# Expert picking of the first token block: one softmax over eight heads, one set of digit instructions, token parts on ScalarE and GpSimd

## The reference

```
q = (xblk @ w_q).reshape(PEER_BLOCK, PEER_HEADS, 2, PEER_DK // 2)   # 8 heads
s1 = einsum('thd,kd->thk', q[:, :, 0], k1); s2 = einsum('thd,kd->thk', q[:, :, 1], k2)   # 128 keys each
t1, i1 = top_k(s1, 16); t2, i2 = top_k(s2, 16)
cand = t1[..., :, None] + t2[..., None, :]            # 256 a head
cidx = i1[..., :, None] * 128 + i2[..., None, :]
top, pos = top_k(cand, 16)
eidx = take_along_axis(cidx, pos)
gate = softmax(top)
act = gelu(einsum('td,thkd->thk', xblk, expert_u[eidx]))
out = einsum('thk,thkd->td', gate * act, expert_v[eidx])
```

## Time and profile before

| | us |
|---|---|
| median of 3 runs | 3845.22 |
| lowest and highest | 3839.84, 3849.98 |
| the profiled execution | 3841.5 |
| its span | 3839.8 |
| PE busy in the span | 3232.0 (84%) |
| DVE busy | 1787.3 (47%) |
| DMA, mean over the span | 284 GB/s |

### The profile page before, as it was taken

One profiled execution on the slowest core, in us unless ns is written; L12 is line 12 of the kernel. 1 busy time (PEld: TensorE's weight loads), 2 busy tenths in 40 slices (PEclk: granted clock), 3 DMA queues, 4 the chain that ended last, 5 costly groups with the idle time before them and its releaser, 6 DMA issues.

```text
span 3839.8 us, 51087 instructions
## 1 busy us (share of the span) xinstructions
PE 3232.0 (84%) x18104; PEld 2209.3 (58%) x18104; DVE 1787.3 (47%) x4186; ACT 622.4 (16%) x1638; POOL 816.7 (21%) x921
## 2 busy tenths in 40 slices
PE   8999999999998899999899999978765666665564
PEld 7767777777776679999788888745410000000000
DVE  2396655555554310003633333358965444444544
ACT  1001222222221100001011110122221111111111
POOL 1000222211211000000122222223233333333332
PEclk9999999999999889999999999979865555555555
DMA  5433323323331358887799999999999999999997
GB/s 188 152 124 126 112 92 108 114 93 107 111 107 68 127 178 294 295 288 259 272 419 419 417 419 417 418 404 417 386 371 418 418 416 418 417 416 414 415 416 305
DMA packets 201143, 1089.73 MB, mean 284 GB/s; under 512 B 27088, under 2 KB 68944, under 8 KB 73616
## 3 DMA queue, kind: packets, MB, share of 16 engines
q0 software_dynamic: 92160, 671.13, 42.6%
q1 hardware_dynamic: 101760, 394.97, 28.9%
q10 hardware_dynamic: 7120, 22.22, 1.5%
HBM read 1056.59 MB, written 31.65 MB: 283 GB/s over the span
## 4 chain that ended last, share of the span: by engine, by line
PE 54%; DMA 29%; DVE 10%; issue 5%; ACT 1%; POOL 1%; DVEq 0%; SPq 0%; ACTq 0%; POOLq 0%
PE psum L497 24%; DMA branches<-in_peer_u,idx 24%; PE psum L561 15%; DMA ring<-in_peer_u,idx 4%; DVE branches L1801 2%; PE psum L921 2%; DVE branches L1355 2%; DVE ring L1801 1%; PE psum L634 1%; PE psum L643 1%; PE psum L640 1%; PE psum L739 1%; PE psum L338 1%; PE psum L620 1%; PE psum L904 1%
## 5 line engine op out<-in xcount | busy, mean ns | idle before, releaser
L1801 DVE CUSTOM_DVE_ANT_0 ring<-ring,psum 128x1024 f32<-128x1024 f32 x480 | 566.8, 1218 | 644.9 <-DMA ring<-in_peer_u,idx 602.8
L497 PE MATMUL psum<-hT,ring 128*128 128x128 f32 (+2 forms) x4800 | 802.5, 328 | 29.1 <-DMA ring<-in_w_glu 10.6
L497 PEld LDWEIGHTS psum<-hT,ring 128*128 128x128 f32 x4800 | 720.0, 196 | 104.0 <-issue 31.5
L904 PE MATMUL psum<-shared,selb 24*128 24x512 bf16 x1280 | 304.0, 524 | 460.8 <-DVE dots L1801 455.9
L904 PEld LDWEIGHTS psum<-shared,selb 24*128 24x128 bf16 x1280 | 56.5, 96 | 1025.9 <-DVE dots L1801 933.0
L561 PE MATMUL psum<-hT,ring 128*128 128x320 f32 x2112 | 626.4, 436 | 9.4 <-DMA ring<-in_w_att 7.8
L561 PEld LDWEIGHTS psum<-hT,ring 128*128 128x128 f32 x2112 | 382.9, 192 | 142.1 <-issue 15.2
L1215 ACT ACTIVATE ge<-dots 128x1 f32<-128x1 f32 x320 | 94.4, 295 | 1493.6 <-DVE dots L1801 1493.6
L497 PE MATMUL psum<-branches,ring 128*128 128x128 f32 (+1 forms) x2048 | 297.1, 304 | 6.4 <-ACT shared L1151 6.4
L1801 DVE CUSTOM_DVE_ANT_0 branches<-branches,psum 128x1024 f32<-128x1024 f32 x160 | 189.0, 1219 | 237.4 <-DMA branches<-in_peer_u,idx 236.0
L497 PEld LDWEIGHTS psum<-branches,ring 128*128 128x128 f32 x2048 | 287.6, 193 | 10.0 <-issue 10.0
(11 more groups left out here) (385 smaller groups left out, 3343.0 us busy)
## 6 DMA issues: line engine op xcount, KB each, us to landing
ring<-in_w_merge SPq DMA_DIRECT2D x160, 1024.0 KB, 5.2
ring<-in_w_head SPq DMA_DIRECT2D x64, 1024.0 KB, 4.9
ring<-in_w_outp SPq DMA_DIRECT2D x32, 1024.0 KB, 7.0
ring<-in_w_pq SPq DMA_DIRECT2D x32, 1024.0 KB, 8.2
ring<-in_w_att SPq DMA_DIRECT2D x24, 1024.0 KB, 5.5
ring<-in_w_mem SPq DMA_DIRECT2D x16, 1024.0 KB, 5.1
ring<-in_w_glu SPq DMA_DIRECT2D x16, 1024.0 KB, 6.5
out_qkv_out<-ring ACTq DMA_DIRECT2D x16, 520.5 KB
```

The lines of the kernel that those rows point to most:

```text
L497: last = mat(out, ring[:, j, (k0 + kt) * P:(k0 + kt + 1) * P], src[:, kt, :], start=kt == 0, stop=kt == kts - 1)
L904: last = mat(ps[q][:, :], selb[32 * q:32 * q + 24, j, :], hb[32 * q:32 * q + 24, g_, :], start=True, stop=True)
L1801: v.tensor_tensor_reduce(out=u, in0=u, in1=x, scale=1.0, scalar=0.0, op0=ALU.mult, op1=ALU.add, accum_out=dots[:, g_, j, half_:half_ + 1]) ...
```

## The change

It has four parts. (1) Both digits are handled by one set of the three instructions, over twice the elements. (2) The exponential, sum, reciprocal and product of the softmax leave the heads: part 2 writes the 16 best sums into `gfull`, and when all eight heads are through, `gates_in` subtracts the maxima, ScalarE makes one exponential over all heads, and `gates_out` writes the gates over them. `picked` now counts a head when its indices are made, and once more for the gates. Both blocks use it. (3) TensorE transposes the index lists after two tiles, multiplies the third, and then transposes the gates; gathers need the index lists alone (`lists_ready` 1 instead of 2). The lists are transposed a second time into a bank nobody reads, to count `summed`. (4) The first block's token parts: ScalarE copies all of the tokens out of PSUM at m = 0 and makes the three parts by one instruction each at m = 0, 4 and 8; GpSimd makes the two subtractions between; the store stands behind m = 8. VectorE's `rest_pair` is used by the second block alone.

```diff
-            for k in range(3):
+            for k in range(2):
                 merge_tile(0, k)
             pe.wait_ge(picked, PH)
-            nc.tensor.transpose(ps[0][:, 0:P], tk0["efull"][:, 0, :], ident[:]).then_inc(summed, SLOTS)
+            nc.tensor.transpose(ps[2][:, 0:P], tk0["efull"][:, 0, :], ident[:]).then_inc(summed, SLOTS - 1)
+            nc.tensor.transpose(ps[0][:, 0:P], tk0["efull"][:, 0, :], ident[:]).then_inc(lists_turned, 1)
+            merge_tile(0, 2)
+            pe.wait_ge(picked, PH + 1)
             nc.tensor.transpose(ps[1][:, 0:P], tk0["gfull"][:, 0, :], ident[:]).then_inc(lists_turned, 1)
+            nc.tensor.transpose(ps[2][:, P:2 * P], tk0["gfull"][:, 0, :], ident[:]).then_inc(summed, 1)
             for k in range(3, 5):
                 merge_tile(0, k)
...
-                pe.wait_ge(picked, 2 * PH)
                 pe.wait_ge(turned_read, 8)
                 for n, name in enumerate(("efull", "gfull")):
+                    pe.wait_ge(picked, 2 * PH + 1 + n)
                     for t in two:
                         w = P if t == 0 else NS
                         last = nc.tensor.transpose(ps[6 + n][:, t * P:t * P + w], tk1[name][0:w, t, :], ident[0:w, 0:w])
-                last.then_inc(lists_turned, 1)
+                    last.then_inc(lists_turned, 1)
...
+            def first_parts(m):
+
+                act.wait_ge(rest_ready, m)
+                if m == 0:
+                    for q in range(4):
+                        act.wait_ge(turned, q + 1)
+                        last = fn(hres0[:, q * 512:(q + 1) * 512], ps[q], ACT.Copy)
+                    last.then_inc(part_taken, 1)
+                    act.wait_ge(part_taken, 1)
+                fn(parts[:, m, :], hres0, ACT.Copy).then_inc(part_taken, 1)
+                if m == 2:
+                    act.wait_ge(part_taken, 4)
+                    act.dma_start(hparts[0:P], parts[:, :, :]).then_inc(parts_out, 16)
...
-                if m == 0:
-                    for n in two:
-                        split_pair(n, 0, 2 * n, N0, (2 * n, 2 * n + 1))
-                    store_parts(1, 0)
-                else:
+                if m:
                     take_scores0(m - 1)
-                if m >= 5 and m % 2:
-                    soften((m - 5) // 2)
+                if m in (0, 4, 8):
+                    first_parts(m // 4)
...
-            soften(6)
-            soften(7)
-            for n in range(3):
-                gate(0, n)
+            gate(0, 0)
+            gate(0, 1)
+            soften(0)
+            gate(0, 2)
...
-                for n in softened(s):
-                    soften(PH + n)
+                if s == LISTS_AT:
+                    soften(1)
...
-                    v.tensor_tensor(gx, top, top[:, :, 0:1].to_broadcast([P, units, TOPK]), ALU.subtract).then_inc(soft_in, 1)
...
-                    for x in two:
-                        st(v.tensor_tensor(eq, fdig[:, x, :].unsqueeze(2).to_broadcast([P, units * TOPK, TOPK]),
-                                           iota16[:].unsqueeze(1).to_broadcast([P, units * TOPK, TOPK]), ALU.is_equal))
-                        st.wait()
-                        e4 = eq.rearrange("p (t k) r -> p t k r", t=units)
-                        st(v.tensor_tensor(e4, e4, tk["i16"][:, x].unsqueeze(2).to_broadcast([P, units, TOPK, TOPK]), ALU.mult))
-                        st.wait()
-                        st(v.tensor_reduce(e12[:, x, :], eq, AX, ALU.add))
-                        st.wait()
-                    st(v.scalar_tensor_tensor(tk["efull"][:, :, at_], e12[:, 0, :].rearrange("p (t k) -> p t k", t=units),
-                                              float(NK), e12[:, 1, :].rearrange("p (t k) -> p t k", t=units), ALU.mult, ALU.add))
-                    dve.wait_ge(soft_out, first + h + 1)
-                    st(v.tensor_reduce(gsum.rearrange("p t n -> p (t n)"), gx, AX, ALU.add))
+                    st(v.tensor_tensor(eq, fdig.rearrange("p x n -> p (x n)").unsqueeze(2).to_broadcast([P, 2 * units * TOPK, TOPK]),
+                                       iota16[:].unsqueeze(1).to_broadcast([P, 2 * units * TOPK, TOPK]), ALU.is_equal))
                     st.wait()
-                    st(v.reciprocal(gsum, gsum))
+                    e4 = eq.rearrange("p (x k) r -> p x k r", x=2 * units)
+                    i4 = tk["i16"].rearrange("p x t k -> p (x t) k")
+                    st(v.tensor_tensor(e4, e4, i4.unsqueeze(2).to_broadcast([P, 2 * units, TOPK, TOPK]), ALU.mult))
                     st.wait()
-                    v.tensor_tensor(tk["gfull"][:, :, at_], gx, gsum.to_broadcast([P, units, TOPK]), ALU.mult).then_inc(picked, 1)
-                    dve.wait_ge(picked, first + h + 1)
+                    st(v.tensor_reduce(e12.rearrange("p x n -> p (x n)"), eq, AX, ALU.add))
+                    st.wait()
+                    v.scalar_tensor_tensor(tk["efull"][:, :, at_], e12[:, 0, :].rearrange("p (t k) -> p t k", t=units),
+                                           float(NK), e12[:, 1, :].rearrange("p (t k) -> p t k", t=units), ALU.mult, ALU.add)\
+                        .then_inc(picked, 1)
+
+            def gates_in(tk, n):
+
+                units = tk["units"]
+                for t in range(units):
+                    top = tk["gfull"][:, t, :].rearrange("p (h k) -> p h k", h=PH)
+                    gx = tk["cand"][:, t, 0:PH * TOPK].rearrange("p (h k) -> p h k", h=PH)
+                    last = v.tensor_tensor(gx, top, top[:, :, 0:1].to_broadcast([P, PH, TOPK]), ALU.subtract)
+                last.then_inc(soft_in, 1)
...
+            def gates_out(tk, n):
+                units = tk["units"]
+                dve.wait_ge(soft_out, n + 1)
+                for t in range(units):
+                    gx = tk["cand"][:, t, 0:PH * TOPK].rearrange("p (h k) -> p h k", h=PH)
+                    st(v.tensor_reduce(tk["gsum"][:, t * PH:(t + 1) * PH, 0], gx, AX, ALU.add))
+                st.wait()
+                st(v.reciprocal(tk["gsum"], tk["gsum"]))
+                st.wait()
+                for t in range(units):
+                    gx = tk["cand"][:, t, 0:PH * TOPK].rearrange("p (h k) -> p h k", h=PH)
+                    last = v.tensor_tensor(tk["gfull"][:, t, :].rearrange("p (h k) -> p h k", h=PH), gx,
+                                           tk["gsum"][:, t * PH:(t + 1) * PH, :].to_broadcast([P, PH, TOPK]), ALU.mult)
+                last.then_inc(picked, 1)
 
             for h in range(PH):
                 for part in range(4):
                     topk_part(tk0, h, part)
+            gates_in(tk0, 0)
+            v.memset(ps[5], 0.0).then_inc(dotted[1], SLOTS)
             dve.wait_ge(lists_turned, 1)
             v.tensor_copy(eT[:, 0:N0], ps[0][:, 0:N0]).then_inc(lists_ready, 1)
+            gates_out(tk0, 0)
+            st(v.memset(ps[4], 0.0))
+            dve.wait_ge(lists_turned, 2)
             v.tensor_copy(gT[:, 0:N0], ps[1][:, 0:N0]).then_inc(lists_ready, 1)
-            st(v.memset(ps[4], 0.0))
-            v.memset(ps[5], 0.0).then_inc(dotted[1], SLOTS)
...
                 elif LAST_TOPK <= s < LISTS_AT:
                     for n in ((0, 1), (2, 3), (4,), (5,), (6,), (7,))[s - LAST_TOPK]:
                         topk_part(tk1, 6 + n // 4, n % 4)
+                    if s == LISTS_AT - 1:
+                        gates_in(tk1, 1)
+                elif s == LISTS_AT:
+                    gates_out(tk1, 1)
                 elif s == LISTS_AT + 1:
-                    dve.wait_ge(lists_turned, 2)
+                    dve.wait_ge(lists_turned, 3)
                     v.tensor_copy(eT[:, N0:], ps[6][:, 0:N1]).then_inc(lists_ready, 1)
+                    dve.wait_ge(lists_turned, 4)
                     v.tensor_copy(gT[:, N0:], ps[7][:, 0:N1]).then_inc(lists_ready, 1)
...
+            for m in two:
+                pool.wait_ge(part_taken, m + 2)
+                if m:
+                    pool.wait_ge(rest_ready, m)
+                g.tensor_tensor(hres0, hres0, parts[:, m, :], ALU.subtract).then_inc(rest_ready, 1)
...
-            pool.wait_ge(lists_ready, 2)
+            pool.wait_ge(lists_ready, 1)
             with pool.Fori(0, 8) as i:
                 gather_pair(i)
-            pool.wait_ge(lists_ready, 4)
+            pool.wait_ge(lists_ready, 3)
```

52 lines of the change are left out of this document (22 added, 30 removed).

## The result

| | before | after |
|---|---|---|
| median of 4 runs each, us | 3847.09 | 3817.76 |
| lowest and highest | 3839.84, 3849.98 | 3815.53, 3822.07 |
| the profiled execution | 3841.5 | 3818.61 |
| its span | 3839.8 | 3816.9 |
| PE, DVE, ACT busy | 3232.0, 1787.3, 622.4 | 3227.9, 1770.1, 605.3 |

The ratio is 0.9928, with a 95% interval of 0.9911 to 0.9945; a later measurement, with 15 runs of the kernel before and 5 of the changed one, gave 0.9944 (0.9931 to 0.9958). The change makes the kernel faster by 0.6 to 0.7%, 21 to 28 us. The forecast was 16 us, and the time lies under its range.

The account below looks back on a forecast made before the run. The DMA flow, hardly resting after the first expert rows and thin from 2720 to 2820, bounds the kernel. 16.2 - 0.5 (contention) - 0.5 (thinner start) + 0.5 (second block) = about 16 us off 3845.2: 3829.2 us, range 3820 to 3839.

Parts of the forecast that it names:

- A head in 8.19 us, no stall in head 0: First block's picking on VectorE: 1.14 us saved a head from 9.33, and head 0's 4.0 us stall gone; 13.1 us.
- The list at 1860.3: End of the first block's picking: head 7's index list ready at about 1860.3 us.
- the contention: GpSimd's second subtraction beside VectorE's picking in the first block: cost 0 to 1.5 us, taken as 0.5.
- Handing over: From list to gather: TensorE waits for VectorE, 4.9 us go; first gather at about 1862.8, 18.7 us earlier.
- DMA decides, not TensorE: Flow after the first gather: DMA side sets the gain, 16 us; the rival, TensorE deciding, 10 us, chance 0.2.
- What survives of it: Of the 18.7 us earlier flow, 2.5 us go to one weight tile now fetched in it; net 16 us.
- the weight tile and the thinner start: Start of the DMA flow: 2.5 us for a 1 MB tile now in it, 0.5 us for its thinner start.
- Token parts: First block: VectorE's eight subtractions worth nothing, GpSimd's 3.8 us each; store one microsecond late, hidden.
- Second block, 0.5 us: Second block's picking: 4.5 us saved against 4.1 us for the gates of all heads; net 0.4, taken as 0.5.
- Only the heads in the thin stretch count, four of eight: Second block: savings of 0.54 and 0.6 us a head count in four heads only, 4.5 us.
- the gates' step: One step of the second block's expert loop: VectorE subtracts, waits for the exponential, makes all heads' gates; costs 4.1 us.
- Rival (b): Thin stretch shrinks by 4.5 us, exponential's wait hidden, tile's 2.5 us paid by idle DMA: 3823 us, chance 0.12.

Follow-up runs that it names:

- first_two_sets: The changed kernel with two digit sets for each head of the first block, as before the change; 3824.25 us, ratio 0.9953.
- own_parts: The changed kernel with the first block's token parts back on ScalarE and VectorE, nothing on GpSimd; 3817.69 us, ratio 0.9935.
- hold: The changed kernel, but GpSimd asks for no expert rows until the gates are ready as well as the lists; 3823.86 us, ratio 0.9952.
- both_shorter: The changed kernel with the first block's token parts back on ScalarE and VectorE and the third tile ahead of the lists' transposes; 3820.66 us, ratio 0.9937.
- first_only: The changed kernel with the second block's picking put back (two digit sets, a softmax for each head); 3827.08 us, ratio 0.9963.
- extra_low: The changed kernel with the digit comparison made three times instead of once in heads 0 to 3 of the second block; 3831.08 us, ratio 0.9970.
- extra_high: The changed kernel with the digit comparison made three times instead of once in heads 4 to 7 of the second block; 3831.83 us, ratio 0.9976.
- soft_early: The changed kernel with the second block's exponential one step of the expert loop earlier on ScalarE; 3822.20 us, ratio 0.9950.
- second_gates: The kernel before with only the second block's softmax taken out of the heads, two digit sets kept; 3837.36 us, ratio 0.9992.

## Why the prediction was wrong

- **A head in 8.19 us, no stall in head 0**: right, 8.15 us and no wait. The combined digit set saves 0.57 us a head (first_two_sets), where 0.54 had been priced.
- **The list at 1860.3**: on the clock of the kernel before it was 1862.4 (1860.51 + 1.89). The difference is the contention, which the 1860.3 left out and the sum had too small: 2.4 us (own_parts) where I took 0.5, with a bound of 1.5. I spread the price of the earlier trace rows over instructions as a slowdown. It is a wait for the end of one GpSimd instruction, so the bound was that instruction's length, 4 us, which the prediction had worked out itself (3.8).
- **Handing over**: right. TensorE waits for VectorE (7.20 us), from list to gather 2.84 us instead of 2.5. The first gather is 16.3 us earlier, where 18.7 less 0.5 had been forecast.
- **DMA decides, not TensorE**: right, by hold and by the pair own_parts and both_shorter. The first token was 10.2 us earlier (1891.59 and 1879.45, less the 1.9), in the forecast's 9 to 12.
- **What survives of it**: first_only has a lead of 12.0 us at the end, 14.2 us by its ratio. The forecast for this part was 15.2. The terms for the weight tile and the thinner start, 3.0 us together, would have left 13.3 of the 16.3 us; 1.3 us more are gone. By its index copies the lead of first_only, counted from the last scores, is 15.8 us at the 1st, 14.3 at the 15th, 13.0 at the 18th and 12.0 at the last. The loss is spread over the flow in steps smaller than the scatter, so no run shows the two terms or the rest singly.
- **Token parts**: "VectorE's eight subtractions are worth nothing" was right. GpSimd's subtraction took 4.07 us (3.8 forecast). Nobody waited for the store.
- **Second block, 0.5 us**: this step failed. Its size is 9 us on top of the first block's change (first_only), 4 to 6 in lead and 6.5 to 8.1 by ratio in the kernel before. Two things were wrong. "Only the heads in the thin stretch count, four of eight" took a full DMA share for slack on VectorE, but the dots had stopped waiting for rows 100 us earlier, and all eight heads count (extra_low, extra_high, and the size of the gain): 8 x (0.64 + 0.70) = 10.7 us saved instead of 4.5; 0.64 is two sets of 3.88 against one of 3.24, and 0.70 what stood behind L1722 in a head (0.63) with L1702 (about 0.1). And the 4.1 us charged for the gates' step were too much: of the 10.7 us 8.9 came out, which leaves about 1.8 for it, and 2.42 of the 4.1 were the wait for the exponential, without which nothing was gained (soft_early). second_gates points the same way, with a lead of 4.2 us out of 5.6 saved. Rival (b) had the sign of it, with too small a price (3823, a chance of 0.12).
- **The base**: the forecast was set on a median of three runs, 3845.2. In the five later measurements (9 to 21 runs each) the kernel before has medians of 3840.4 to 3842.6. So 3 to 5 us of the missing 11.4 are that base. It is no gain of the change: against those, the changed kernel is 21 to 25 us faster. The leads explain 5.2 us of the miss (20.9 against 15.7), and what is then left, 1 to 4 us, is no more than the intervals of the medians.

In one sum, as leads at the end of the flow: first block 12.0 (15.2 forecast), second block 8.9 (0.5 forecast), together 20.9 us against 15.7.
